# Ranks of a mixture-of-experts layer read back and added in the experts' last pairs, by a folded identity

## What is computed

```python
    _, idx = lax.top_k(scores + prm['b_router'], TOP_K)      # 8 of 128 experts a token
    sel = jnp.take_along_axis(scores, idx, axis=-1)
    gate = sel / jnp.sum(sel, axis=-1, keepdims=True) * ROUTED_SCALE
    ...
        h = jax.nn.silu(xb @ prm['w_e1'][e]) * (xb @ prm['w_e3'][e])
        yb = (h @ prm['w_e2'][e]) * w[:, None]
        return acc.at[tok].add(yb), None
    ...
    shared = (jax.nn.silu(xt @ prm['w_s1']) * (xt @ prm['w_s3'])) @ prm['w_s2']
    return shared + routed
...
    y = layer_norm(ALPHA * h + moe_ffn(h, prm), prm['ln2_g'], prm['ln2_b'], LN_EPS)
```

## Time and profile before

| | us |
|---|---|
| time, median of 3 (lowest, highest) | 2023.21 (2018.51, 2024.14) |
| the profiled execution, its own time | 2027.02 |
| its span | 2025.3 |
| PE busy | 1784.4 (88%) |
| VectorE, ScalarE, GpSimd busy | 632.6, 389.1, 362.4 |
| HBM read and written | 522.52 MB, 41.42 MB |

### The profile page before, as it was taken

How to read it: one execution, slowest core, us unless ns; L and a number is a source line. 1 busy time by engine, 2 the same in 40 slices (tenths; PEclk the granted TensorE clock), 3 DMA queues, 4 the chain that set the end, 5 groups by cost and what they waited for, 6 DMA issues and landing times. The chain is left out here.

```text
span 2025.3 us, 29331 instructions
## 1 busy us (share of the span) xinstructions
PE 1784.4 (88%) x10614; PEld 1052.9 (52%) x10614; DVE 632.6 (31%) x1516; ACT 389.1 (19%) x916; POOL 362.4 (18%) x529
## 2 busy tenths in 40 slices
PE   7999997879999998899988978888787878888887
PEld 6857776778778884465533333333333333333332
DVE  1387754774214311431111111111111111111127
ACT  0114544442120100211111111111111111111102
POOL 1000001888870000001111011111111111011100
PEclk8999998999999999999999899999999999899898
DMA  4433312001242324269999999999999999999976
GB/s 118 145 138 104 105 32 48 3 21 36 60 152 80 113 81 187 106 252 402 420 421 419 408 418 407 410 419 405 410 399 409 405 404 406 392 409 417 404 294 251
DMA packets 160782, 532.04 MB, mean 263 GB/s; under 512 B 22061, under 2 KB 88927, under 8 KB 110205
## 3 DMA queue, kind: packets, MB, share of 16 engines
q1 hardware_dynamic: 138971, 488.63, 61.3%
q0 software_dynamic: 20640, 41.23, 5.4%
q10 hardware_dynamic: 1098, 1.18, 0.2%
HBM read 522.52 MB, written 41.42 MB: 278 GB/s over the span
## 5 line engine op out<-in xcount | busy, mean ns | idle before, releaser
L1965 PE MATMUL bank<-arena 128*64 128x512 f32 x2048 | 504.7, 650 | 146.3 <-DMA arena<-in_w_e 146.3
L1965 PEld LDWEIGHTS bank<-arena 128*64 128x64 f32 x2048 | 157.6, 149 | 488.9 <-issue 488.9
L1983 PE MATMUL bank<-arena 128*64 128x512 f32 x1024 | 233.8, 598 | 0.0
L2212 DVE TENSOR_TENSOR arena<-bank,arena 128x256 f32<-128x256 f32 x64 | 27.2, 425 | 578.4 <-ACT arena L2057 578.4
L1835 POOL DMA_INDIRECT arena<-h_rows,index x66 | 66.9, 1013 | 776.5 <-DVE index L2087 727.6
L1425 PE MATMUL bank<-arena 128*128 128x276 f32 x768 | 183.0, 397 | 7.3 <-ACT arena L1527 3.1
L1425 PEld LDWEIGHTS bank<-arena 128*128 128x128 f32 x768 | 145.3, 190 | 41.1 <-ACT arena L1527 3.5
L1201 PE MATMUL bank<-arena 64*64 64x64 f32 (+2 forms) x2816 | 124.2, 243 | 28.5 <-DVE arena L1314 15.3
L2057 ACT ACTIVATE arena<-bank 128x256 f32<-128x256 f32 x64 | 24.7, 385 | 603.9 <-PE bank L1965 603.9
L1201 PEld LDWEIGHTS bank<-arena 64*64 64x64 f32 x2816 | 109.3, 138 | 35.3 <-DVE arena L1314 16.2
L1983 PEld LDWEIGHTS bank<-arena 128*64 128x64 f32 x1024 | 67.8, 136 | 110.9 <-issue 109.7
(11 more groups left out here) (332 smaller groups left out, 1850.0 us busy)
## 6 DMA issues: line engine op xcount, KB each, us to landing
arena<-in_w_e SPq DMA_DIRECT2D x384, 1024.0 KB, 14.0
arena<-in_w_in SPq DMA_DIRECT2D x50, 512.0 KB, 4.1
arena<-routed_rows SPq DMA_DIRECT2D x8, 2048.0 KB, 22.9
arena<-in_w_mem_kv SPq DMA_DIRECT2D x4, 1024.0 KB, 5.9
arena<-in_cache_mem_k SPq DMA_DIRECT2D x8, 512.0 KB, 5.1
arena<-in_cache_mem_v SPq DMA_DIRECT2D x8, 512.0 KB, 6.6
arena<-in_w_out SPq DMA_DIRECT2D x2, 2048.0 KB, 13.0
arena<-in_w_s SPq DMA_DIRECT2D x3, 1024.0 KB, 10.6
```

The lines of the kernel that those rows point to most:

```text
L1965: mm = pe.matmul(p_gu[t * S:(t + 1) * S, :], xt[:, v, c, t * S:(t + 1) * S], w13[2 * v + t][:, :, c, :], start=(c == 0), stop=(c == KD - 1))
L1983: mm = pe.matmul(p_y[h][t * S:(t + 1) * S, :], hidT[:, j, t * S:(t + 1) * S], w2[2 * v + t][:, j, h * 512:(h + 1) * 512], start=(j == 0), ...
```

## The change

- The shared expert's down product and `ALPHA * h` (a product of `hT` with `ALPHA` times the identity) are made for each (tile, half) in pairs 12 to 21 of the experts' loop, in bank 7 (`base`); VectorE copies the sum to `res`. w_s2 is loaded ahead of the loop. `h_rows` is not read back.
- A rank's rows are loaded in 32 transfers of 64 partitions with 8 KB each: partitions 0 to 63 hold one pair of ranks, 64 to 127 another, of the same 64 tokens. The first are issued while the last pairs run, behind waits for the scatters and for the buffers that they overwrite. The samples' ranks come in four transfers of 32 partitions.
- PE adds them by products with `m.fold`, two identities of 64 above one another: one product adds two ranks, and the two halves of a tile's tokens go to the two column halves of the array (`fold`). All eight ranks are added so; VectorE adds none.
- The layer norm takes the form of the first one in the program (L2109 to L2121 before): ScalarE squares and takes the root, VectorE does the rest with two fused operations. The tiles' order is 0, 1, 2, samples, 3. `stage_combine` is gone and its work stands at the end of `stage_mix_experts`.

```diff
+O_LOW = ((O_HT, O_HT + PART), (O_WEXP[0], O_WEXP[0] + PART), (O_WEXP[2], O_WEXP[2] + PART), (O_WEXP[3], O_WEXP[3] + PART))
+O_HIGH = ((O_WEXP[1], O_WEXP[1] + PART), (O_WEXP[0] + 2 * PART, O_WEXP[1] + 2 * PART),
+          (O_WEXP[2] + 2 * PART, O_WEXP[3] + 2 * PART), (O_XG, O_XTE))
+LAST = (0, 1, 2, NTT - 1, 3)
...
@@ SP
+            sp.wait_ge(s_oh, 1)
+            sp.dma_start(w2s, io["w_s2"][0].rearrange("(k p) n -> p k n", p=P)).then_inc(sem("shared_down_loaded"), 16)
...
-            for i, (c0, n) in enumerate(TILES[:-1]):
-                sp.dma_start(res[:, i, :], io["h_rows"][c0:c0 + n, :]).then_inc(sem("h_rows_back"), 16)
...
+            def ranks(i, place, first, x, s):
+
+                for a in range(2):
+                    t0 = TILES[i][0] + a * HD
+                    sp.dma_start(m.arena[x * HD:(x + 1) * HD, place[i][a]:place[i][a] + PART].rearrange("p (k d) -> p k d", k=2),
+                                 routed[t0:t0 + HD, first:first + 2, :]).then_inc(s[i], 16)
+
+            def low(i):
+                for x in range(2):
+                    ranks(i, O_LOW, 2 * x, x, s_low)
+
+            def high(i, x):
+                ranks(i, O_HIGH, 4 + 2 * x, x, s_high)
+
+            sp.wait_ge(s_base, 2 * NTT + 13)
+            sp.wait_ge(s_out[1], (16 * NP // 2) * count)
+            low(0)
+            sp.wait_ge(s_xt, NP * count)
+            low(1)
+            sp.wait_ge(s_out[0], (16 * NP // 2) * count + 16)
+            high(0, 0)
+            sp.wait_ge(s_yv, NP * count)
+            high(1, 0)
+            sp.wait_ge(s_gu, NP * count)
+            low(2)
+            sp.wait_ge(s_out[1], (16 * NP // 2) * count + 16)
+            high(0, 1)
+            high(1, 1)
+            sp.wait_ge(s_y, NP * count)
+            for x in range(2):
+                high(2, x)
+            for t in range(TS):
+                sp.dma_start(spart[t * BS * 4:(t + 1) * BS * 4, :], routed[SEQ + 1 + t:NT:SB].rearrange("b (x k) d -> b x (k d)", x=4))                  .then_inc(sem("sample_ranks_loaded"), 16)
+            low(3)
+            sp.wait_ge(s_xt, NP * count + 1)
+            sp.wait_ge(s_in[1], (16 * NP // 2) * count + 16)
+            for x in range(2):
+                high(3, x)
...
@@ PE
+            def base(t, h):
+
+                n, cols = RES_ROWS[t], slice(t * P, (t + 1) * P)
+                bank = m.ps[7][0:n, :]
+                for j in range(2):
+                    pe.matmul(bank, sact[:, j, cols] if n == P else ssam[:, j, :], w2s[:, j, h * 512:(h + 1) * 512],
+                              start=(j == 0), stop=False)
+                for k in range(4):
+                    mm = pe.matmul(bank[:, k * P:(k + 1) * P], hT[:, 4 * h + k, cols] if n == P else hsam[:, 4 * h + k, :], alpha,
+                                   start=False, stop=(k == 3))
+                mm.then_inc(s_bp, 1)
+
+            def fold(i, place, s):
+
+                high = place is O_HIGH
+                pe.wait_ge(s[i], 64)
+                for h in range(2):
+                    for k in range(2):
+                        for a in range(2):
+                            part = m.at(place[i][a], PART)
+                            mm = pe.matmul(final_bank(i, h)[a * HD:(a + 1) * HD, :], m.fold[:, :],
+                                           part[:, k * D + h * 512:k * D + (h + 1) * 512],
+                                           start=(not high and k == 0), stop=(high and k == 1))
+                if high:
+                    mm.then_inc(s_all, 1)
...
+                            with pe.If(i > 5):
+                                pe.wait_ge(s_base, 2 * i + (v + 1))
+                                for t in range(NTT):
+                                    with pe.If(i < 7 + t):
+                                        with pe.If(i > 5 + t):
+                                            base(t, v)
...
@@ DVE
+                            with dve.If(i > 2):
+                                dve.wait_ge(s_bp, 4 * i + (u + 1))
+                                dve.tensor_copy(m.arena[:, ds(2 * D * i + (O_RES - 6 * D + 512 * u), 512)], m.ps[7][:, :])\
+                                   .then_inc(s_base, 1)
...
-STAGES = (stage_load, stage_front, stage_wkv_merge, stage_mix_experts, stage_combine)
+STAGES = (stage_load, stage_front, stage_wkv_merge, stage_mix_experts)
```

More of the change, by code:

```diff
@@ L1796, in _ @@
                         load(r, NP - 2 + v, v, 2 * v)
[L1798 to L1803 removed]
+            routed = io["routed_rows"].rearrange("(t k) d -> t k d", k=TOPK)
@@ L1985, in _ @@
                         mm.then_inc(s_y, 1)
[L1986 to L1992, removed]
+                        with pe.If((NP // 2) * r + i < 11):
+                            if v == 0:
+                                with pe.If(i < 3):
+                                    shared_late(1, i * THIRD, i + 2)
+                            else:
+                                with pe.If(i < 4):
+                                    with pe.If(i > 2):
+                                        shared_late(0, 2 * THIRD, 5)
+                            with pe.If(i > 5):
[4 more added lines that the diff above has]
+                                            base(t, v)
+            pe.wait_ge(s_idx, NP * count + 3)
+            pe.wait_ge(s_xt, NP * count + 1)
+            pe.wait_ge(s_hc, NP * count)
+            pe.wait_ge(s_yv, NP * count + 1)
+            pe.wait_ge(s_ya, NP * count + 1)
+            fold(0, O_LOW, s_low)
+            fold(1, O_LOW, s_low)
+            fold(0, O_HIGH, s_high)
+            fold(1, O_HIGH, s_high)
+            fold(2, O_LOW, s_low)
+            fold(2, O_HIGH, s_high)
+            pe.wait_ge(s_fmean, 1)
+            pe.wait_ge(sem("sample_ranks_loaded"), 16 * TS)
+            for h in range(2):
+                for k in range(2):
+                    mm = pe.matmul(final_bank(NTT - 1, h)[0:BS * TS, :], fold32,
+                                   spart[:, k * D + h * 512:k * D + (h + 1) * 512], start=(k == 0), stop=(k == 1))
+            mm.then_inc(s_all, 1)
+            fold(3, O_LOW, s_low)
+            fold(3, O_HIGH, s_high)
         @block.scalar
@@ L2203, in shared_samples @@
                     dve.tensor_copy(ssam[:, j, :].rearrange("p (b t) -> p b t", b=BS), sample_cols(sact[:, j, SEQ:NT]))
+                for k in range(KD):
+                    last = dve.tensor_copy(hsam[:, k, :].rearrange("p (b t) -> p b t", b=BS), sample_cols(hT[:, k, SEQ:NT]))
+                last.then_inc(s_base, 13)
+            dve.tensor_scalar(alpha, m.ident[:, :], ALPHA, None, ALU.mult)
+            dve.tensor_reduce(fold32.rearrange("p (b t) -> p b t", b=BS), m.ident[:, :].rearrange("p (t b x) -> p b t x", t=TS, b=BS),
+                              AX.X, ALU.add)
             count = rounds(dve)
@@ L2290, in _, with final_mean @@
+            def final_mean(g, i):
+                n, st, zi = RES_ROWS[i], fstats[0:RES_ROWS[i], i, :], res[0:RES_ROWS[i], i, :]
+                dve.wait_ge(s_all, g + 1)
                 for h in range(2):
                     cols = slice(h * 512, (h + 1) * 512)
-                    for j in range(2):
-                        rows = sact[:, j, i * P:(i + 1) * P] if i < NTT - 1 else ssam[:, j, :]
-                        pe.matmul(bank(i, h)[0:n, :], rows, w2s[:, j, cols], start=(j == 0), stop=False)
@@ L2313, in _ @@
[L2313 to L2331 removed]
+                    dve.scalar_tensor_tensor(out=zi[:, cols], in0=zi[:, cols], scalar=1.0, in1=final_bank(i, h)[0:n, :],
+                                             op0=ALU.mult, op1=ALU.add, accum_out=st[:, h:h + 1])
```

175 lines of the change are left out of this document (65 added, 110 removed).

## The result

The changed kernel takes **2044.37 us** (median of four runs, 2043.10 to 2044.68); the kernel before took 2022.52 us beside it (four runs, 2018.51 to 2024.14). The ratio is 1.0098, with a 95% interval of 1.0076 to 1.0119: slower by 1.0%, or 2023.21 x 0.0098 = 19.8 us. The forecast was slower by 10.8. The median lies 0.4 us above the upper end of the range, 2044.0; by the ratio it is 2043.0, just inside. So the direction and the mechanism came as forecast, and the size was not quite twice what I worked out.

The account below looks back on a forecast made before the run. PE's adding after the loop gives way to the 64-partition rank stream: last rank 2021.3, plus fold 6.1, norm 6.0, output 2.7 gives 2036.1, 10.8 us slower; on the median 2034.0 us. Range 2020 to 2044, 8 in 10: 1999 to 2044.

Parts of the forecast that it names:

- What bounds, and what is moved: After the experts' loop: PE's adding of ranks bounds now; its 51 us go, and the new readback stream bounds instead.
- Base in the loop at no cost: Experts' loop, pairs 12 to 21: 2.6 us more PE work a pair, 15.6 below the average 16.65, costs nothing.
- rival (c): Experts' loop: base work lengthens it by up to 5 us, 2039; sign: pairs above 16.7 us; chance 0.05.
- Order on SP: Loads around the loop's end: no wait starves the queue, ranks stream from 1942.4, 13.6 us earlier than today's.
- rival (d): Loop's end: reads don't start in the loop because an SP wait comes late; 2008.3 us, chance 0.02.
- The price of 64 partitions: Readback of ranks: 17.83 MB to 64 partitions a transfer at 233 GB/s, 76.5 us, last rank at 2021.3.
- my 233: Readback of ranks: the rate in GB/s taken from the sample_vectors load, with 191 and 425 as the ends.
- the estimate beside my sum: Readback of ranks: by the skill page's limit of 218 GB/s the stream would take 5 us more.
- Behind the last rank: Kernel's end: last fold with its wait 6.1 us, layer norm 6.0, output 2.7, ending at 2036.1.
- (a): Readback: narrow transfers run at full rate, five layer norms then follow one another; 2001.8 us, chance 0.26.
- (b): Readback: engines out of step write both halves, rate between, 300 GB/s; 2016.2 us, chance 0.12.
- The decision point of 271 GB/s: Readback: the change gains if the stream's mean rate is above 271 GB/s.

Follow-up runs that it names:

- experiment 7: The twelve base products of each of the ten pairs left out: of the changed kernel 2045.38 us, of a_wide 2005.66 us.
- a_wide: Changed kernel with each ranks' load writing all 128 partitions (1 MB), the fold adding neighbours, loads in another order: 2003.39 us, 0.9889 of the kernel before.
- experiments 1, 2 and 4: Ranks' loads to all 128 partitions in the changed kernel (2003.39 us), to 64 in the kernel before (2066.63 us), to even or odd 64 in the changed (2004.12 us).
- a_narrow_order: Changed kernel with its 64-partition loads kept, only the order of loads and folds that of a_wide: 2046.02 us, 1.0108 of the kernel before.
- a_even_odd: a_narrow_order with the two loads of a token half going to the even and the odd partitions: 2004.12 us, 0.9903 of the kernel before.
- experiment 5: Samples' loads sent to every fourth partition, source read as four groups of eight: in the changed kernel 2042.56 us, in a_wide 2013.77 us.

## Why the prediction was right, and where its size was off

**What bounds, and what is moved.** Confirmed: PE's and VectorE's adding after the loop gave way to the stream of ranks, and all of PE's waits there are for `routed_rows`.

**Base in the loop at no cost.** Right, by experiment 7. A pair costs 3.0 us more and not 2.6, which still leaves it below 16.65. The ten pairs with the work follow one another by (1240.88 - 1092.14) / 9 = 16.5 us (starts of their base products), below the 16.7 that I had given as the sign of rival (c), which is out.

**Order on SP.** Right in that the loop's reads start in time (rival (d) is out): the first are ordered at 1927.36, no wait starves the queue, and the weights are through at 1935.9, when the last pair's product starts. That is 6.5 us ahead of my 1942.4, of which 3.5 are an earlier start of the loop (897.72 for 901.24). The other 3.0 are partly a matter of where the line is drawn: ranks share the queues with weights from 1927.36 on, so some of them had moved by 1935.9. I had not seen the price on the other side: the last pair becomes 7 us longer and the last scatter lands 13.7 us after its issue. Both lie beside a stream that goes on without a gap (share 1.01 to 1.04), so I take them to cost nothing at the end; no run shows that by itself. In `a_wide`, with a stream twice as fast, the same waits do leave gaps.

**The price of 64 partitions.** The mechanism was right; experiments 1, 2 and 4 show it. The term was mis-sized. By the windows 0.87 + 2.32 + 8.60 = 11.8 MB are moved from 1935.9 to 1990, 218 GB/s, and 6.9 MB in the 40.3 us up to 2030.3, 171 GB/s. With my 233 the two stretches would have taken 50.6 and 29.5 us; they took 54.1 and 40.3. So 3.5 us come from the plateau's rate, which I took from a window of half a microsecond (238 at 1.02 in the earlier trace rows), in which loads of L1125, ordered from 330.15 on, may have had a part. Why the half microsecond ahead of it was faster no run shows; the long streams had neither rate. And **10.8 us come from the last 40 us**, where I had let the same rate go on: there the samples' loads stand in the stream (145 GB/s), and then the DMA engines end at different times (shares 0.80 and 0.43). The same unevenness stood in my rows, 0.78 and 0.13 at the end of the weight stream; I used it for the start of the ranks and not for their end. The remaining 1.2 us are a balance of bytes: I left out three output stores and the samples' store, 1.7 MB, and some 1 MB of ranks (an estimate from the windows) had moved before 1935.9. Sum: -6.5 + 3.5 + 10.8 + 1.2 = +9.0, and 2021.3 became 2030.3.

The plateau's 218 GB/s is the limit that the Trainium skill's page "SBUF — State Buffer", section "Door 1: The DMA port swizzle", gives for partitions 0 to 63; the estimate beside my sum, 5 us more, was nearer to the plateau than the sum itself. The reading of 233 that I said agreed with it lay 7% above that limit.

**Behind the last rank.** Fold 3.65 instead of 6.1 (the wait before it was 1.27 us and not 5, and its 16 instructions took no longer than those of the earlier trace rows), norm 2034.01 to 2039.88, 5.9 instead of the 6.0 that the earlier trace rows gave, output 3.0 instead of 2.7. Together 9.0 - 2.45 - 0.1 + 0.3 = 6.75 of the span's 6.8 (2042.9 for 2036.1). The remaining 2 us between spans and ratio are that the profiled execution of the kernel before was slower than its median, 2027.02 for 2023.21.

**Rivals (a) and (b).** (a) fell with the changed kernel's first window, and came true, to 1.6 us, when experiment 1 took its condition away: 2003.4 for 2001.8. The chain of five norms held, 5.8 us each for my 6.0. That the sum came so near is in part luck: its stream was full from 1942.4 on, where that of `a_wide` has gaps, but the loop of `a_wide` also began 5.4 us earlier than the one I worked from (895.85 for 901.24). (b), engines out of step, would have given 300 GB/s; no stretch of 10 us of a narrow stream was above 244, not even with two queues. The decision point of 271 GB/s lies between 219 and 423, and the sign turned between these two; no run came nearer to it.

## What to carry to other kernels

When a transfer is given a new shape, price the partitions that it writes, and look at how they lie: the bytes, the DMA share and the number of loads were the same at 2046 us (`a_narrow_order`) and at 2004 us (`a_even_odd`), and only GB/s at full share told them apart. Look at the outermost dimension of its source as well, which an edit of the target can change unseen (experiment 5). A sum that rests on a stream has an end with a rate of its own (small loads among large ones, engines that finish apart), and that end was three quarters of what the rate was wrong by here. If a reduction over partitions is to be folded by a matrix anyway, the matrix can just as well add neighbours, which lets each load reach all 128 partitions; `a_wide`, at 2003.4 us, is faster than both kernels.

## What the runs showed of the hardware that I had not expected

64 partitions in one half (0 to 63 or 64 to 127): 213 to 219 GB/s at full share; 64 even or odd ones: 412; all 128: 421 to 425. Lower and upper half from two queues at once: 231. A scatter issued into the narrow stream landed after 13.7 us, into the wide one of `a_wide` after 8.7 (1946.75 to 1955.47), into an idle queue after 3.4. And loads to 32 partitions at a distance of four, of which I had expected the full rate, ended on four DMA engines while most others had nothing left; the wide kernel was some 10 us slower with them.
